# A transformer block in float32: x handed over transposed, value tiles before the root, blocks normalised behind them

## The reference

```python
def rms_norm(x, g):
    xf = x.astype(jnp.float32)
    y = xf * lax.rsqrt(jnp.mean(xf * xf, axis=-1, keepdims=True) + RMS_EPS)
    return (y * g.astype(jnp.float32)).astype(x.dtype)
...
    hn = rms_norm(x, g_pre_mix)
    proj = hn @ w_in
    mq, mk, mv, fq, fk, fv, f_logit, cvb, cvc, cvh = jnp.split(proj, SPLIT_IDX, axis=-1)
```

## Time and profile before

| | us |
|---|---|
| median of 3 runs | 575.63 (575.08 to 576.1) |
| the profiled execution | 576.57 |
| its span | 574.8 |
| TensorE busy | 567.5 (99%) |
| VectorE busy | 471.5 (82%) |
| ScalarE busy | 319.7 (56%) |
| GpSimd busy | 110.4 (19%) |

### The profile page before, as it was taken

The page is one execution under the profiler, slowest core; times in us unless marked ns, Lnnn a source line. Parts: engine busy times, 40 slices in busy tenths (PEclk is TensorE's granted clock), DMA queues, the critical chain, the costliest instruction groups (busy, mean ns, idle before and its releaser), DMA issues.

```text
span 574.8 us, 9664 instructions
## 1 busy us (share of the span) xinstructions
PE 567.5 (99%) x3372; PEld 502.8 (87%) x3372; DVE 471.5 (82%) x791; ACT 319.7 (56%) x539; POOL 110.4 (19%) x129
## 2 busy tenths in 40 slices
PE   8999999999999999999999999999999999999996
PEld 6988888888888888899999999999999988888884
DVE  5647888888797954799888988988898788888787
ACT  5625765766555645575545546454554565547762
POOL 3020001103220000000324242332324002233100
PEclk9999999999999999999999999999999999999999
DMA  8274334346312471302323223242322359999743
GB/s 331 85 214 136 91 105 132 95 141 185 110 48 100 147 299 68 111 38 75 144 76 131 88 75 144 73 145 74 144 75 81 138 188 268 269 211 199 167 146 146
DMA packets 23144, 78.92 MB, mean 137 GB/s; under 512 B 2972, under 2 KB 2972, under 8 KB 23114
## 3 DMA queue, kind: packets, MB, share of 16 engines
q1 hardware_dynamic: 16716, 57.44, 28.2%
q0 software_dynamic: 6304, 21.00, 16.1%
q10 hardware_dynamic: 94, 0.09, 0.0%
HBM read 71.16 MB, written 4.22 MB: 131 GB/s over the span
## 4 chain that ended last, share of the span: by engine, by line
PE 99%; DVE 0%; POOL 0%; issue 0%; DVEq 0%; ACT 0%; POOLq 0%
PE bank L1666 11%; PE bank L1668 11%; PE bank L1667 11%; PE bank L1951 8%; PE bank L1950 8%; PE bank L1949 8%; PE bank L1957 7%; PE bank L2019 6%; PE bank L2017 6%; PE bank L2015 6%; PE bank L1960 3%; PE bank L1720 3%; PE bank L1827 3%; PE bank L1815 2%; PE bank L1805 1%; PE bank L1803 1%
## 5 line engine op out<-in xcount | busy, mean ns | idle before, releaser
L1950 PE MATMUL bank<-tok_lo,form_hi 128*128 128x256 f32 x320 | 90.6, 283 | 0.0
L1951 PE MATMUL bank<-tok_hi,form_lo 128*128 128x256 f32 x320 | 90.6, 283 | 0.0
L1949 PE MATMUL bank<-tok_hi,form_hi 128*128 128x256 f32 x320 | 90.5, 283 | 0.0
L1666 PE MATMUL bank<-hn,w_hi 128*128 128x512 f32 (+1 forms) x200 | 76.6, 383 | 0.0
L1668 PE MATMUL bank<-hn,w_lo 128*128 128x512 f32 (+1 forms) x200 | 75.0, 375 | 0.0
L1667 PE MATMUL bank<-hn,w_hi 128*128 128x512 f32 (+1 forms) x200 | 74.6, 373 | 0.0
L1949 PEld LDWEIGHTS bank<-tok_hi,form_hi 128*128 128x128 f32 x320 | 60.9, 190 | 1.9
L1951 PEld LDWEIGHTS bank<-tok_hi,form_lo 128*128 128x128 f32 x320 | 61.1, 191 | 0.0
L1950 PEld LDWEIGHTS bank<-tok_lo,form_hi 128*128 128x128 f32 x320 | 61.0, 191 | 0.0
L2015 PE MATMUL bank<-dw_hi,da_hi 128*128 128x512 f32 x154 | 59.9, 389 | 0.0
L2019 PE MATMUL bank<-dw_hi,da_lo 128*128 128x512 f32 x154 | 59.9, 389 | 0.0
(11 more groups left out here) (206 smaller groups left out, 1397.0 us busy)
## 6 DMA issues: line engine op xcount, KB each, us to landing
raw<-in_w_gate_units SPq DMA_DIRECT2D x22, 512.0 KB, 3.6
raw<-in_w_up_units SPq DMA_DIRECT2D x22, 512.0 KB, 4.5
raw<-in_w_in_units SPq DMA_DIRECT2D x21, 512.0 KB, 3.3
down_x<-in_w_down POOLq DMA_DIRECT2D x15, 512.0 KB, 9.7
down_y<-in_w_down SPq DMA_DIRECT2D x10, 512.0 KB, 9.2
raw<-in_w_out SPq DMA_DIRECT2D x8, 512.0 KB, 3.2
q_lh<-q_hl POOLq DMA_DIRECT2D x12, 256.0 KB, 2.8
down_x<-in_w_down SPq DMA_DIRECT2D x5, 512.0 KB, 3.9
```

The costliest lines, as they stand in the source:

```text
L1666: nc.tensor.matmul(out_ap, sh, mh, start=first, stop=False)
L1949: nc.tensor.matmul(out_ap, sh, mh, start=first and k == 0, stop=False, skip_group_check=True)
L1950: nc.tensor.matmul(out_ap, sh, ml, start=False, stop=False, skip_group_check=True)
L1951: mm = nc.tensor.matmul(out_ap, sl, mh, start=False, stop=k == HK - 1, skip_group_check=True)
```

## The change

x is handed over a second time, transposed (`x_t`, 8 blocks of 128 features by 512 tokens), and `g_pre_mix` as one column for each block. The transposes and the broadcast of the norm's weights are gone. ScalarE rounds x times g (`features_hi`), VectorE takes its rest (`features_lo`), and all four value tiles are made from that, each in a bank of its own (4 to 7), block by block as x and the weights arrive; the root of each token is multiplied in when a value tile is evacuated. Its evacuation on VectorE is three instructions and one for the gates, where it was one and a copy; tiles 1 to 3 have it inside steps 0 to 2 of the attention stage.

Plain x is still loaded, behind the values' operands, for the sums of squares. The roots are put on all partitions by four transposes (`row_scales`); then VectorE normalises the eight blocks (`normalise`), ScalarE rounds them over the old ones (`tokens_hi`), and the rests are taken by VectorE, those of blocks 3, 5 and 7 by GpSimd. GpSimd also rounds weight units 3, 4 and 5 and takes the rests of 4 and 5, ahead of the bias loads and of the swap of pair 0, which stood first in its list. The query and key tile of pair 0 are interleaved by blocks. In step 0 of the attention stage the three filler products come ahead of the logits. The diff, cut (longer runs of removed lines are those of the kernel before, above):

```diff
-XT_BANKS = ((2, 3), (4, 5))
-G_BANKS = (6, 7)
-REL_BANKS = (2, 3)
-WARM = (4, 2)
+V_BANKS = (4, 5, 6, 7)
+REL_BANKS = (0, 1)
+R_BANK = 3
+WARM = 12
...
-V_GROUPS = (0, 1, 2, 5)
+V_GROUPS = (0, 1, 2, 3)
...
-V_CHUNKS = ((0, 2), (2, 5), (5, 8))
+V_CHUNKS = ((0, 1), (1, 4), (4, 8))
+X_CHUNKS = ((0, 2), (2, 4), (4, 8))
+LATE_CHUNK = 2
+POOL_UNITS = (3, 4, 5)
+POOL_RESTS = (4, 5)
+POOL_BLOCKS = (3, 5, 7)
...
+            load_turned(0)
             load_values(0)
             load_values(1)
+            load_turned(1)
             load_values(2)
-            load_open(2)
-            load_open(3)
+            load_turned(2)
             load(3, unit(w_in_units, 0))
-            load(4, unit(w_in_units, 1), 1)
+            for t in range(TT):
+                load_open(t)
+            load(4, unit(w_in_units, 1), 0)
...
+            def rounded(u):
+
+                pool.wait_ge(raw_in[u % RAW], 16 * (u // RAW + 1))
+                nc.gpsimd.tensor_copy(split_slot(u)[0][:, :, :], staged(u)).then_inc(pool_hi_done, 1)
+
+            def rest(u):
+
+                hi, lo = split_slot(u)
+                pool.wait_ge(pool_hi_done, POOL_UNITS.index(u) + 1)
+                nc.gpsimd.tensor_tensor(lo[:, :, :], staged(u), hi[:, :, :], ALU.subtract).then_inc(pool_lo_done, 1)
+
+            rounded(3)
+            rounded(4)
+            rest(4)
+            for k in POOL_BLOCKS:
+                pool.wait_ge(hn_hi_done, KT + k + 1)
+                nc.gpsimd.tensor_tensor(hn_lo[:, k, :], xt[:, k, :], hn_hi[:, k, :], ALU.subtract
+                                        ).then_inc(hn_pool_lo, 1)
             pool.wait_ge(rel_copied, 2)
             pool.dma_start(rel_rows.ap(), rel_row[:, :]).then_inc(rel_out, 16)
+            rounded(5)
+            rest(5)
 
...
             for p in range(MOBA_PAIRS + 1):
                 load_bias(p)
-                if p >= 1:
-                    swap(p)
+                swap(p)
...
...
+            def features_hi(k):
+
+                chunk = next(n for n, (k0, k1) in enumerate(X_CHUNKS) if k0 <= k < k1)
+                act_e.wait_ge(xt_in[chunk], 16)
+                nc.scalar.activation(hn_hi[:, k, :], xt[:, k, :], ACT.Copy, scale=g_feat[:, k:k + 1]
+                                     ).then_inc(hn_hi_done, 1)
+
+            def tokens_hi(k):
+
+                if k < KT - 1:
+                    act_e.wait_ge(v_used, k + 1)
+                else:
+                    act_e.wait_ge(proj_done, V_GROUPS[-1] + 1)
+                act_e.wait_ge(xn_done, k + 1)
+                nc.scalar.copy(hn_hi[:, k, :], xt[:, k, :]).then_inc(hn_hi_done, 1)
 
...
...
+            act_e.wait_ge(g_in, 16)
+            for k in range(KT):
+                features_hi(k)
+            for t in range(TT):
+                squares_of(t)
             act_e.wait_ge(rel_done, 1)
             nc.scalar.copy(rel_row[:, 0:SEQ], bank[0:N_MOBA, REL_BANKS[0], :]).then_inc(rel_copied, 1)
             nc.scalar.copy(rel_row[:, SEQ:REL], bank[0:N_MOBA, REL_BANKS[1], 0:REL - SEQ]).then_inc(rel_copied, 1)
-            evac_hi(V_GROUPS[0])
-            tokens_hi(2)
-            split(3)
-            evac_hi(V_GROUPS[1])
-            tokens_hi(3)
             nc.scalar.preload_act_table_set("natural_log_exp_and_others")
-            split(4)
-            evac_hi(V_GROUPS[2])
-            split(5)
-            evac_hi(group(0, 0))
+            for k in range(KT):
+                tokens_hi(k)
             split(6)
-            evac_hi(group(0, 1))
-            evac_hi(V_GROUPS[3])
+            for t in range(2):
+                evac_hi(V_GROUPS[t])
+            for j in range(2):
+                evac_hi(group(0, j))
+            for t in range(2, TT):
+                evac_hi(V_GROUPS[t])
...
+            def features_lo(k):
+
+                dve.wait_ge(hn_hi_done, k + 1)
+                nc.vector.scalar_tensor_tensor(out=hn_lo[:, k, :], in0=xt[:, k, :], scalar=g_feat[:, k:k + 1],
+                                               in1=hn_hi[:, k, :], op0=ALU.mult, op1=ALU.subtract
+                                               ).then_inc(hn_lo_done, 1)
+
+            def row_scales(t):
+
                 inverse_std(SQ1, t)
...
+                if t == 0:
+                    dve.wait_ge(ones_set, 1)
+                nc.vector.tensor_scalar(r_tok[:, t, :], r_tok[:, t, :], rstd[:, SQ1, t:t + 1], None, ALU.mult
+                                        ).then_inc(r_tok_done, 1)
+
+            def normalise(k):
+
+                if k == 0:
+                    dve.wait_ge(hn_lo_done, KT)
+                    dve.wait_ge(r_turned, 1)
+                nc.vector.scalar_tensor_tensor(out=xt[:, k, :], in0=xt[:, k, :], scalar=g_feat[:, k:k + 1],
+                                               in1=bank[:, R_BANK, :], op0=ALU.mult, op1=ALU.mult).then_inc(xn_done, 1)
+
+            def tokens_lo(k):
+
+                dve.wait_ge(hn_hi_done, KT + k + 1)
+                nc.vector.tensor_tensor(hn_lo[:, k, :], xt[:, k, :], hn_hi[:, k, :], ALU.subtract
+                                        ).then_inc(hn_lo_done, 1)
 
...
+                    src = bank[:, V_BANKS[p], :]
+                    for m in range(MOBA_PAIRS):
+                        last = nc.vector.scalar_tensor_tensor(
+                            out=v_moba[:, m, p, :, DH:P],
+                            in0=src[:, P * m:P * (m + 1)].rearrange("p (h d) -> p h d", h=2),
+                            scalar=rstd[:, SQ1, p:p + 1], in1=v_moba[:, m, p, :, 0:DH], op0=ALU.mult,
+                            op1=ALU.subtract)
+                    last.then_inc(v_lo_done, 1)
+                    nc.vector.tensor_scalar(f_tok[:, p, :], src[:, MOBA_W:V_COLS], rstd[:, SQ1, p:p + 1], None,
+                                            ALU.mult).then_inc(proj_read, 1)
...
-            normalise(0)
-            normalise(1)
-            tokens_lo(0)
+            features_lo(0)
             split(0)
-            tokens_lo(1)
+            features_lo(1)
+            split(1)
+            features_lo(2)
+            features_lo(3)
             dve.wait_ge(rel_hi_done, 2)
             nc.vector.tensor_tensor(relb_hl[:, 1, :], relb[:, :], relb_hl[:, 0, :], ALU.subtract).then_inc(rel_lo_done, 1)
-            split(1)
+            for k in range(4, KT):
+                features_lo(k)
             split(2)
-            normalise(2)
-            normalise(3)
+            split(3)
+            for t in range(TT):
+                row_scales(t)
+            normalise(0)
+            for k in range(KT):
+                if k + 1 < KT:
+                    normalise(k + 1)
+                if k not in POOL_BLOCKS:
+                    tokens_lo(k)
+            evac_lo(group(0, 0))
+            evac_lo(group(0, 1))
             evac_lo(V_GROUPS[0])
...
 
...
+                if g == 0:
+                    split(6)
+                if g < TT - 1:
+                    evac_lo(V_GROUPS[g + 1])
...
+            def row_scales():
+
+                pe.wait_ge(r_tok_done, TT)
+                for t in range(TT):
+                    mm = nc.tensor.transpose(bank[:, R_BANK, P * t:P * (t + 1)], r_tok[:, t, :], ident[:, :])
+                mm.then_inc(r_turned, 1)
 
...
+            for u in range(V_UNITS):
+                pe.wait_ge(wv_hi_done, u + 1)
+                for k in range(*V_CHUNKS[u]):
+                    pe.wait_ge(hn_hi_done, k + 1)
+                    for t in range(TT):
                         v_mm(t, k, hn_hi, wv_hi, k == 0, False)
...
+                    pe.wait_ge(hn_lo_done, k + 1)
+                    for t in range(TT):
+                        v_mm(t, k, hn_lo, wv_hi, False, False)
+                    if u < LATE_CHUNK:
+                        v_weight_rests(u, (k,))
             relative_rows()
...
+            v_weight_rests(LATE_CHUNK, (4, 5))
+            row_scales()
+            v_weight_rests(LATE_CHUNK, (6, 7))
+            pe.wait_ge(rel_copied, 2)
+            proj_step(group(0, 0), V_UNITS, 0)
+            for k in range(1, KT):
+                proj_step(group(0, 0), V_UNITS, k)
+                if k >= 2:
+                    proj_step(group(0, 1), V_UNITS + 1, k - 2)
+            for k in range(KT - 2, KT):
+                proj_step(group(0, 1), V_UNITS + 1, k)
...
+                items = filler_at(g)
+                if g == 0:
+                    for G, k in items:
+                        proj_step(G, G - 1, k)
+                    items = []
```

More of the change, by code:

```diff
@@ L144, in unit_group, with rests_before, reads_with @@
 def unit_group(u):
-    return u if u < V_GROUPS[-1] else u + 1
+    return u + 1
+def rests_before(u):
+    return u - sum(v < u for v in POOL_RESTS)
+def reads_with(G):
+    if G in V_GROUPS:
+        return G + 3
+    return G - TT + 1 if G < TT + 2 else G + 1
 def slot_groups(u):
@@ L348, in hybrid_block @@
         g_in = sem("g_in")
-        g_done = sem("g_done")
+        xt_in = [sem(f"xt_in{n}") for n in range(len(X_CHUNKS))]
+        ones_set = sem("ones_set")
```

(31 more changed lines are left out.)

192 lines of the change are left out of this document (54 added, 138 removed).

## The result

The changed kernel takes 585.28 us (584.87 to 586.2) beside 575.87 (575.08 to 576.59) for the kernel before: ratio 1.0164, 95% interval 1.0151 to 1.0177. I had forecast 577.0 and a range up to 578.8; the loss is 9.4 us, not 1.4. The profiled execution has a span of 583.6, 8.8 over before's 574.8.

A forecast was written before the change was run, and what follows sets the result against it. TensorE bounds the kernel (99% of the chain). A 3.8 us head start was to be lost to the swap wait and VectorE's longer queue: 57.7 less 56.27 is +1.4, added to median 575.63: 577.0 us, range 573.3 to 578.8.

The forecast's parts named there:

- product of the group after next: Attention stage's first steps: this product waits for the next query tile's evacuation, starting at 57.7 against 56.27, +1.4 us.
- The swap's landing: Ahead of first logits: second swap, queued behind two 256 KB bias loads, lands in 3.3 us; first logits at 43.5.
- A: Experiments' theory, not the prediction's: the swap is late because two bias loads stand ahead in GpSimd's queue; no chance given.
- The swap's issue: GpSimd's queue behind block 7 (34.3): relative rows, unit 5, bias issues, first swap; second swap goes out at 40.1.
- the list of arrivals: Opening's loads: turned x, values and weights, then plain x; fourth plain tile in at 19.7, next weights at 21.0.
- rival 4: Opening: GpSimd and VectorE hold each other up, or plain x lands late; 578.5 to 579.5, chance 0.15.
- GpSimd's prices: GpSimd before the swap: block rest 1.3 us, unit 5's rounding 1.04, its rest 2.4 to 2.5, or 3.5.
- TensorE's own share: Opening: TensorE alone shrinks by 4 us, is short of work about 2.1, ends the key tile at 38.65.
- VectorE behind the first logits: First attention steps: VectorE's queue takes 9.9 us against 9.1, then 4.2 and 0.1 to the later product.
- a lower clock would hide there: After TensorE's idle 2.8 us before first logits: slower products hide in the wait for VectorE; no cost added.

The follow-up runs named there:

- e3: Changed kernel with the first four bias loads (pairs 0 and 1) issued by SyncE, ahead of unit 9's load, instead of GpSimd: 584.31 us, ratio 1.0148.
- g1: e3 with one more move: the relative rows' DMA right behind GpSimd's rest of unit 4, so the bias loads leave earlier: 580.1 us, ratio 1.0075.
- e1: Changed kernel with GpSimd issuing pair 0's swap ahead of pair 0's bias loads instead of behind them: 582.66 us, ratio 1.0114.
- f2: Changed kernel with GpSimd's rest of unit 4 held until VectorE has scaled all four roots: 585.15 us, ratio 1.0157.
- e4: Changed kernel with VectorE's rests of value tiles 1 to 3 and unit 6 taken ahead of the first logits: 584.41 us, ratio 1.0152.
- f4: e4 with 44 unread transposes of the identity in TensorE's queue ahead of the first logits: 582.46 us, ratio 1.0109.
- f1: Changed kernel with pair 0's bias loads and unit 9's load held until the swap landed, pair 1's bias until the first logits: 585.48 us, one run.
- g4: Kernel before with relative rows sent once copied and four bias loads ahead of the first swap, behind the query tile's copy: 582.19 us, ratio 1.0115.

## Why the prediction was wrong

Its steps against the trace:

| step | predicted | measured |
|---|---|---|
| first value matmul | 5.6 | 6.45 |
| normalising starts | 24.4 | 26.55 |
| block 7's rest done | 34.3 | 36.75 |
| key tile's last product | 38.65 | 41.1 |
| second swap issued | 40.1 | 42.58 |
| first logits | 43.5 | 50.71 |
| product of the group after next | 57.7 | 65.02 |
| against before | +1.4 | +8.8 |

*The swap's landing: the step that failed.* I took "3.3, the top of the swap's 2.8 to 3.3, where bias loads take 3.4 to 4.1". It took 8.0: 4.7 of the 7.2 us by which the first logits missed. The rows were those of a swap with nearly nothing beside it, and I carried them to a place where, by my own order of GpSimd's queue, two bias loads stood ahead and two behind, and where the rest of unit 5 frees the load of unit 9. (The second half of before's first swap itself took 3.3 and was in at 39.3, not 38.9.) I wrote down the queue and priced only the issues. The trace of before had a row for a crowded swap, which I didn't look for: a later pair's, beside a load of x and two of weights. The DMA view of before, from 125 to 135 us (all transfers, then the swap's issues, size and median landing):

```profile
DMA packets 852, 3.04 MB, mean 304 GB/s; under 512 B 109, under 2 KB 109, under 8 KB 852
...
q_lh<-q_hl POOLq DMA_DIRECT2D x2, 256.0 KB, 6.9
```

There it hides; its 6.9 us would have put the first logits at 47. The cause is shown in two parts: e3 against g1 shows what is under way in another queue (7.9 and 4.2), and the changed kernel against e1 what stands ahead in the swap's own (8.0 and 5.7). A alone, which would have left 3.3 right for a swap at the head of the queue, is out by e1 and e3. How the 4.7 us divide between the two is not settled, as they overlap.

*The swap's issue, 2.5 us late.* 0.85 of it is in the opening. The first values were cast at 5.89 where I had 5.0, and ScalarE's first block waited for the norm weights till 5.56, a 4 KB load, 4.7 us to land, that I had not put on the list of arrivals at all; the cast, done at 6.40, is what the first matmul waited for. 1.3 more stands ahead of the turned root, 1.02 of it TensorE's wait for the fourth scaling: rival 4's place and mechanism (2.36 us beside 2.38 of GpSimd's subtraction), though in other executions the same lock cost TensorE 0 to 0.6. The Trainium skill, GPSIMD Engine Reference, section 8, has contention where VectorE has two SBUF inputs or a 2-port mode; this instruction has one SBUF tensor as input and a column as its scalar, so that here it would be the second of these. The trace agrees that VectorE waits for GpSimd, whose own 2.38 us stay as they are in f2, and no run tells the modes apart. I had named this inside rival 4, at 0.15; it should have stood in the sum, since both starts were in my own schedule within a microsecond. The other 0.3 us is spread over the normalising. GpSimd's prices, for which before had only bounds, were right: 1.30 for a block (1.3), 2.39 for unit 5's rest (2.4 to 2.5), 1.07 for its rounding (1.04); from block 7 to the second swap 5.8 us, as predicted.

*TensorE's own share.* It ended the key tile 2.45 us later than predicted, all of it inherited from block 7's rest, which was 2.45 late as well; busy time fell by 3.0 us on the page (567.5 to 564.5).

*VectorE behind the first logits: right.* 14.2 us predicted, 14.3 measured (65.02 less 50.71), the loss then carried unchanged to the end. But the sentence that a lower clock would hide there was right for the wrong stretch: it hides only as long as VectorE is slower. At 0.50 until 54 the clock is as near to binding as VectorE: e4, which relieves VectorE alone, wins 0.9 us, and f4 on top of it 2.0.

*The range.* Its top, 578.8, held rival 4 and no landing over 3.3. The swap's landing had no upper bound in the sum, which is why 6.5 us lie outside. With 8 us of landing and the same chain, my sum is 577.0 + 4.7 = 581.7; the 2.5 us of late issue make 584.2, and the measured median is 585.3. Of the 1.1 us left, 0.2 is before's median, 575.87 in this comparison and 575.63 in my sum; 0.6 is that the spans fall 8.8 apart and the medians 9.4, the profiled execution of before, 576.57, having been 0.7 above its median.

## What to carry to other kernels

When a change moves a small transfer, price its landing by the bytes that will be in flight then, all queues together (here some 0.2 MB a us), give it the head of its own queue, and look for the row of the same transfer at its most crowded, not the one at its old place. A step that is only idle time to one engine (here the last value tile behind the query tile) may be the cover of another's latency: the changed kernel removed that cover and put a megabyte beside the swap at the same time. Transfers whose data are ready early are best sent in an engine's idle time well ahead; that one move gave back 4.2 us.

## What the runs showed of the hardware

- A 256 KB copy from SBUF to SBUF lands in 3.1 us with only its other half beside it (f1), in 4.2 with part of a 512 KB load (g1), and in 7.9 to 9.4 with 1 MB of bias loads and a 512 KB load, whether the bias loads are in its own queue (changed kernel, g4) or in SyncE's (e3). With the same megabyte issued behind it, it lands in 5.7 (e1). These mixes move at 0.19 to 0.25 MB a us, while the loads of the opening ran at 418 GB/s; why the mixes are slower was not tried.
- VectorE's scaling of a 128x128 tile by a column, 0.29 us, takes 2.36 to 2.39 beside a 2.38 us subtraction of GpSimd and ends with it, in all ten executions with this order; GpSimd's time doesn't change. VectorE's normalising steps, with one input in PSUM, kept their 1.40 for two beside GpSimd's 1.30 us block rests.
- A load of 4 KB in 128 rows takes 4.5 to 4.7 us to land in the opening, as long as 195 KB of values.
- In gaps of 4.3 and 6.4 us without a matmul (g4, the changed kernel) TensorE's granted clock fell to 0.50, and the matmuls that followed ran at that level for 3 to 5 us more; 44 unread transposes in the gap kept it at 1.00 and were worth 2 us (f4), though 2.2 us of the gap were left empty. A gap of 2.2 us without them was followed by a fall too, and only behind the first matmuls (g1, from 48 to 50):

```profile
48.00:50.00 2.00, 2.00 (x7) 1.61 (x6) 1.96 (x11) 0.66 (x4) 0.00 (x0) 0.50 0.60 174
```
